# A planner in place of a hand-written schedule for the long convolutions and matrix-memory heads of an encoder layer

## The chip, the cores and the metric

The kernel runs on one core of a Trainium2 chip, in one launch. The metric is the device time of an execution in microseconds; lower is better.

## The reference

The layer normalises its input, projects it, and splits the result in a bidirectional gated long convolution of order 2 (512 channels) and a bidirectional mLSTM with four heads of 128; both go through one output projection, and a gated MLP follows. It is applied to a prompt of 1024 tokens and a sample of 512. The stage that the change touches computes `hyena_mix` and `mlstm_bidir`:

```
def hyena_mix(x1, x2, v, kspec, bias):
    def long_conv(z, ks, d):
        zf = jnp.fft.rfft(z, n=2 * L, axis=1)
        return jnp.fft.irfft(zf * ks[None], n=2 * L, axis=1)[:, :L] + d * z
    z = x1.astype(F32) * long_conv(v.astype(F32), kspec[:, 0], bias[0])
    return x2.astype(F32) * long_conv(z, kspec[:, 1], bias[1])

def mlstm_chunkwise(q, k, v, ig, fg):          # forwards, and once more on the flipped sequence
    a = b_last[..., None] - b + ig
    w_loc = jnp.exp(a - m_loc[..., None])
    kw = k * w_loc[..., None]
    C_loc = jnp.einsum('bhcsk,bhcsv->bhckv', kw, v)
    ...                                        # states C, n are carried from chunk to chunk
    Sm = jnp.einsum('bhctd,bhcsd->bhcts', q, k) * jnp.exp(D - m_t[..., None])
    num = inter[..., None] * jnp.einsum('bhctk,cbhkv->bhctv', q, C_prev) + jnp.einsum('bhcts,bhcsv->bhctv', Sm, v)
    h = num / jnp.maximum(jnp.abs(den), jnp.exp(-m_t))[..., None]
```

The heads are then normalised, multiplied by the gate `o`, and joined with the convolution's output.

## The kernel before, in words

Three stages follow one another. `projections_filters_and_gates` (L434) makes the input projection, the filters' spectra and the gates. `long_convolutions_and_heads` (L1397) is the middle stage. `output_and_mlp` (L2130) does the rest. The first and last order their work with `plan()` (L365), a list scheduler: of several streams of steps it takes at each point the step that can start first by stated costs.

**The convolutions.** A stream `st` is a sequence and half of its 512 channels: 0 and 1 are the prompt's halves (8 blocks of 128 tokens), 2 and 3 the sample's (4 blocks). Each stream goes twice, as round `o` 0 and 1, through one transform; (o, st) is a turn. In a turn:
- `split` (TensorE, L1823, one per block) makes the first part of the transform from `mix_z`, ScalarE copies it to `mix_split` (L1925), and SyncE issues a DMA that shuffles it into `mix_classes` (L1680).
- A `pair` (8 of them for a prompt half, 4 for a sample half) is `forward` (TensorE, L1835), the product with a filter block `mix_kf` (VectorE, three operations, L2009 to L2011; the blocks are loaded by SyncE, L1657, in a ring of three), `inverse` (TensorE, L1846) and a copy to `mix_classes` (ScalarE, L1930). The inverse runs two pairs behind the forward (`lag`).
- After a turn's last copy SyncE shuffles back to `mix_split`, one DMA per block (L1686).
- `join` (TensorE, L1856) and the product with the gate (VectorE, L2019, into `mix_z`; `finish`) end each block. Round 0 goes on with the splits of round 1; round 1 with `turn`, a transposition on TensorE (L1864), a copy on ScalarE (L1942) and a store to `y_scratch` on ScalarE's queue (L1950).

Buffers `z`, `split` and `classes` exist in two slots; the prompt's halves use slot 0 one after the other, the sample's halves share slot 1. The first stage loads z of stream 0, 2 and 3 ahead. z of stream 1 is loaded (`load_z`) when stream 0 is transposed.

**The heads.** There are eight jobs, each of the four heads for the sample (short) and the prompt (long). `load_head` is five loads (SyncE, L1710 to L1714); GpSimd adds the mask (L1799); ScalarE takes exponentials (`weigh_tile`, L1962); `keys` on TensorE transposes k and multiplies q by k (L1876, L1881), four tiles at a time; ScalarE scales the keys (L1973), VectorE weighs the scores (L2032); `link` (TensorE, L1892) and `add_state` (VectorE, L2047 and L2049) carry the states from chunk to chunk; `attend` (TensorE, L1905 and L1906), `age` (ScalarE, L1983) and `combine` (VectorE, L2062 and L2064) make the output; a chain on VectorE normalises it, `turn_head` (L1914) transposes, `scale` (L2111) multiplies and `store_head` (L1728) stores.

**What sets the order.** The eight PSUM banks `vyacc` are taken in turn, in the order of the schedule. A hand-written list, `schedule`, gives one joint order, which every engine follows for its own part: ScalarE's copy of a split, SyncE's shuffle of it and VectorE's product of a forward stand where the `split` or `forward` stands. The turns run (0,0), (0,2), (0,3), (1,0), (1,2), (1,3), (0,1), (1,1); `turn_at` says after which pair a turn is joined; joins and the splits or turns after them alternate at a distance of two blocks. The heads' steps are spread among these by a share of cost, with `gap` credits where the convolutions would stand:

```
        else:
            schedule.append((x[0],) + x[2:])
            credit += share * x[1] if n >= leading else 0
        while at < len(heads) and spent < credit:
            schedule.append((heads[at][0],) + heads[at][2:])
            spent += heads[at][1]
            at += 1
```

Loads hang on steps: a filter block on a `forward`, a gate on a turn's last `join`, the eight output weight blocks (`load_out_weights`, L1734, for the next stage) on the forwards of the last turn, the first outputs for the next stage on the last but one `store_head`.

## Time and profile before

| | us |
|---|---|
| median of 3 runs | 2239.07 (2234.37 to 2241.76) |
| the profiled execution | 2236.85 |
| its span | 2235.0 |
| middle stage on TensorE, first split to last transposition | 726.37 to 1085.05 |

The span lies within the execution's own time; the rest lies around it. TensorE was granted 0.985 of its full clock in the mean over the span. In the rows below TensorE has two parts, PE for matmuls and PEld for the load of weights, which overlaps them; DVE is VectorE, ACT ScalarE, POOL GpSimd, SP SyncE, and a q behind an engine's name is its sequencer or DMA queue. L and a number is a line of the kernel.

### The profile page before, as it was taken

What the parts mean: (1) busy time and instruction counts of PE and PEld (TensorE: products, weight loads), DVE (VectorE), ACT (ScalarE), POOL (GpSimd) and SP (SyncE); (2) the same over time, 40 slices, a digit from 0 to 9 for tenths busy, and PEclk for the clock granted to TensorE, in tenths of its full rate; (3) what the DMA queues carried; (4) which work ended last, traced back from release to release, by engine and by line L of the source; (5) the groups of instructions that cost most, each with busy time, mean ns of one, the idle gap of its engine ahead of it and who ended that gap; (6) DMA issues with size and microseconds to landing.
All of it is one profiled execution on the core that took longest, in us unless ns stands there. A gap on an engine that the chain in (4) does not pass through costs nothing. (4 is left out here: it accounts for less than half of the span.)

```text
span 2235.0 us, 26984 instructions
## 1 busy us (share of the span) xinstructions
PE 2139.8 (96%) x9878; PEld 1775.1 (79%) x9878; DVE 1517.8 (68%) x2078; ACT 934.1 (42%) x1482; POOL 379.4 (17%) x350
## 2 busy tenths in 40 slices
PE   6999999999999899898799999999999999999998
PEld 5788878887877788787688878888888888888886
DVE  6577677555754378577546876569999999655554
ACT  5432233325543445455325543344444444442342
POOL 0221122100110101000000056312353433100000
PEclk9999999999999899899999999999999999999999
DMA  4344444553663866758735278633334443866553
GB/s 152 109 141 139 130 130 131 160 155 133 207 195 118 256 182 208 217 166 236 254 111 191 99 257 302 220 116 107 132 137 141 141 137 104 270 232 195 172 161 118
DMA packets 239164, 377.93 MB, mean 169 GB/s; under 512 B 17816, under 2 KB 143384, under 8 KB 239034
## 3 DMA queue, kind: packets, MB, share of 16 engines
q1 hardware_dynamic: 217802, 300.70, 43.6%
q0 software_dynamic: 19936, 72.10, 8.7%
q10 hardware_dynamic: 1296, 3.41, 0.4%
q8 instruction: 80, 1.31, 0.2%
q14 instruction: 50, 0.41, 0.1%
HBM read 252.08 MB, written 98.11 MB: 157 GB/s over the span
## 5 line engine op out<-in xcount | busy, mean ns | idle before, releaser
L128 PE MATMUL in_acc<-in_h_hi,in_w_hi 128*128 128x512 f32 x464 | 191.0, 412 | 2.6 <-DVE in_h_lo L1175 2.6
L130 PE MATMUL in_acc<-in_h_hi,in_w_lo 128*128 128x512 f32 x464 | 182.0, 392 | 0.0
L129 PE MATMUL in_acc<-in_h_lo,in_w_hi 128*128 128x512 f32 x464 | 181.5, 391 | 0.0
L128 PE MATMUL mlp_bank<-down_d_hi,down_s_hi 128*128 128x512 f32 x462 | 179.7, 389 | 0.0
L129 PE MATMUL mlp_bank<-down_d_lo,down_s_hi 128*128 128x512 f32 x462 | 179.7, 389 | 0.0
L130 PE MATMUL mlp_bank<-down_d_hi,down_s_lo 128*128 128x512 f32 x462 | 179.7, 389 | 0.0
L1057 ACT ACTIVATE in_w_hi<-in_w_raw 128x1024 fp32r<-128x1024 f32 x58 | 61.5, 1060 | 214.5 <-PE in_acc L130 214.3
L128 PE MATMUL mlp_bank<-mlp_s_hi,up_w_hi 128*128 128x512 f32 x352 | 138.8, 394 | 3.1 <-DVE up_w_lo L2956 3.1
L129 PE MATMUL mlp_bank<-mlp_s_lo,up_w_hi 128*128 128x512 f32 x352 | 138.2, 393 | 0.0
L130 PE MATMUL mlp_bank<-mlp_s_hi,up_w_lo 128*128 128x512 f32 x352 | 138.0, 392 | 0.0
L2882 ACT ACTIVATE down_s_hi<-down_s_raw 128x1408 fp32r<-128x1408 f32 x42 | 58.0, 1382 | 167.2 <-PE mlp_bank L130 167.2
L1181 DVE TENSOR_TENSOR in_w_lo<-in_w_raw,in_w_hi 128x1024 fp32r<-128x1024 f32 x58 | 71.1, 1226 | 70.3 <-ACT in_w_hi L1057 70.1
L128 PEld LDWEIGHTS in_acc<-in_h_hi,in_w_hi 128*128 128x128 f32 x464 | 87.8, 189 | 20.8 <-DVE in_h_lo L1175 2.8
L128 PE MATMUL mlp_bank<-mlp_h_hi_t,wide_hi_s 128*128 128x512 f32 x264 | 102.7, 389 | 0.0
L129 PE MATMUL mlp_bank<-mlp_h_lo_t,wide_hi_s 128*128 128x512 f32 x264 | 102.7, 389 | 0.0
L130 PE MATMUL mlp_bank<-mlp_h_hi_t,wide_lo_s 128*128 128x512 f32 x264 | 102.7, 389 | 0.0
L130 PEld LDWEIGHTS in_acc<-in_h_hi,in_w_lo 128*128 128x128 f32 x464 | 87.4, 188 | 19.2
L129 PEld LDWEIGHTS in_acc<-in_h_lo,in_w_hi 128*128 128x128 f32 x464 | 87.8, 189 | 17.4
L130 PEld LDWEIGHTS mlp_bank<-down_d_hi,down_s_lo 128*128 128x128 f32 x462 | 86.7, 188 | 18.2
L128 PEld LDWEIGHTS mlp_bank<-down_d_hi,down_s_hi 128*128 128x128 f32 x462 | 86.7, 188 | 18.0
L1846 PE MATMUL mix_vyacc<-mix_prod,mix_tab 128*128 128x256 f32 x384 | 95.3, 393 | 5.8 <-DVE mix_prod L2011 5.8
L129 PEld LDWEIGHTS mlp_bank<-down_d_lo,down_s_hi 128*128 128x128 f32 x462 | 86.7, 188 | 17.8
(298 smaller groups left out, 5522.4 us busy)
## 6 DMA issues: line engine op xcount, KB each, us to landing
in_w_raw<-arg_w_in_t SPq DMA_DIRECT2D x58, 512.0 KB, 3.6
down_s_raw<-s_scratch SPq DMA_DIRECT2D x42, 704.0 KB, 4.5
up_w_raw<-arg_w_up_t SPq DMA_DIRECT2D x44, 512.0 KB, 3.6
wide_raw<-arg_w_up_t SPq DMA_DIRECT2D x44, 512.0 KB, 3.7
filt_tab<-arg_fwd SPq DMA_DIRECT2D x32, 512.0 KB, 3.8
mix_classes<-mix_split SPq DMA_DIRECT2D x48, 256.0 KB, 8.9
mix_kf<-k_scratch SPq DMA_DIRECT2D x48, 256.0 KB, 4.4
mix_split<-mix_classes SPq DMA_DIRECT2D x48, 256.0 KB, 5.2
```

Source lines behind the costliest of these rows:

```text
L128: pe.matmul(out, w_hi, x_hi, start=first, stop=False, skip_group_check=joins)
L129: pe.matmul(out, w_hi, x_lo, start=False, stop=False, skip_group_check=joins)
L130: return pe.matmul(out, w_lo, x_hi, start=False, stop=last, skip_group_check=joins)
L1057: act.activation(w_hi[b][:, :, :], raw[b][:, :, :], ACT.Copy).then_inc(sem["w_high"], 1)
L1181: dve.tensor_tensor(w_lo[b][:, :, :], raw[b][:, :, :], w_hi[b][:, :, :].bitcast(F32), ALU.subtract).then_inc(sem["w_low"], 1)
L1846: last = pe.matmul(out[:, u, :], tab[s][:, t, u, 1 + i, :], prod[g % 2][:, u, i, :], start=i == 0, stop=i == 1)
L2882: act.activation(s_hi[i % n_own][:, :, :], s_raw[i % 2][:, :, :], ACT.Copy).then_inc(sem["s_high"], 1)
```

## The change

`plan()` gets two more arguments: `takes`, which names for a step the steps that free the PSUM banks it takes, so that a step waits for the bank that was taken eight before, and `rank_of`, which decides between steps that can start at the same time. The middle stage then has no hand-written schedule. Each engine's part is a step of its own with an engine, a time, a delay and the steps that it needs (`work`), in 33 streams; `order`, what `plan()` makes of them, takes the place of `schedule`, and each engine follows its own steps in it. A step of the heads goes before one of the convolutions unless their share is ahead by more than 0.1; on SyncE the convolutions go first.

The turns run in another order (`runs`): the sample halves, the first prompt half, both sample halves' second round, then four pairs of the first prompt half's second round, the eight pairs of the second prompt half's first round, the other four pairs, and the second half's second round. Stream 0 moves to slot 1, stream 1 to slot 0, which the sample halves have first; so `load_z` waits for the transpositions of streams 2 and 3, and the first shuffle of stream 1 for their stores. The first stage's loads ahead follow that. The output weights are loaded when stream 0 is stored and four pairs are left. What each step computes is not changed, nor the number of matmuls of the stage. The ring of filter blocks, the lag and the banks stay. The diff, cut:

```diff
-def plan(streams, work, even=False):
-    clock, done, order, at = {}, {}, [], [0] * len(streams)
+def plan(streams, work, even=False, rank_of=None, takes=None, banks=8):
...
+            if takes:
+                needs = needs + [held[i - banks] for i in range(len(held), len(held) + len(takes(step))) if i >= banks]
             if all(x in done for x in needs):
                 start = max([clock.get(engine, 0.0)] + [done[x] for x in needs])
-                rank = at[n] / len(stream) if even else 0
+                rank = rank_of(n, at, step) if rank_of else at[n] / len(stream) if even else 0
...
+        held += takes(step) if takes else []
...
-                        st, s, half, z = ((0, 0, 0, ahead.z[0]), (2, 1, 0, ahead.z[1][:, 0:nts[1], :]), (3, 1, 1, ahead.z[1][:, nts[1]:, :]))[n - z_from]
+                        st, s, half, z = ((0, 0, 0, ahead.z[1]), (2, 1, 0, ahead.z[0][:, 0:nts[1], :]), (3, 1, 1, ahead.z[0][:, nts[1]:, :]))[n - z_from]
...
-    turns = [(0, 0), (0, 2), (0, 3), (1, 0), (1, 2), (1, 3), (0, 1), (1, 1)]
+    early = n_pairs[0] // 2
+    runs = [(0, 2, 0, n_pairs[2]), (0, 3, 0, n_pairs[3]), (0, 0, 0, n_pairs[0]), (1, 2, 0, n_pairs[2]), (1, 3, 0, n_pairs[3]),
+            (1, 0, 0, early), (0, 1, 0, n_pairs[1]), (1, 0, early, n_pairs[0]), (1, 1, 0, n_pairs[1])]
+    turns = [(0, 2), (0, 3), (0, 0), (1, 2), (1, 3), (0, 1), (1, 0), (1, 1)]
+    pairs = [(o, st, t) for o, st, first, end in runs for t in range(first, end)]
...
-    turn_at = {(0, 0): 12, (0, 2): 16, (0, 3): 20, (1, 0): 28, (1, 2): 32, (1, 3): 36}
+    sharers = {0: [x for x in turns if x[1] < 2], 1: [x for x in turns if x[1] >= 2]}
...
-    def join_all(o, st):
-        nb = len(blocks(st))
-        for b in range(nb + 2):
-            if b < nb:
-                conv.append(("join", 0.9, o, st, b))
-            if b >= 2:
-                conv.append(("split", 0.9, 1, st, b - 2) if o == 0 else ("turn", 0.3, st, b - 2))
-        if o == 1:
-            conv.append(("store", 0, st))
...
-    conv.append(("gap", 3.2))
-    alone = first_pair[0, 1]
-    for g in range(alone):
-        pair_step(g, alone)
-        for turn in turns:
-            if turn_at.get(turn) == g:
-                join_all(*turn)
-                if turn == (1, 0):
...
+        if kind == "load_z":
+            return "SP", 2.8, 4.0, [last_block("turn", 2), last_block("turn", 3)]
+        if kind == "split":
+            o, st, b = a
+            return "PE", 0.87, 0.1, [("finish", 0, st, b)] if o else [("load_z", 1)] if st == 1 else []
+        if kind == "shuffle":
+            o, st, b = a
+            return "SP", 0.72, 3.5, [("copy_split",) + a] + ([last_block("back", 0, st)] if o else [("store", 2), ("store", 3)] if st == 1 else [])
+        if kind == "load_k":
+            return "SP", 0.72, 3.5, [("multiply", a[0] - ring)] if a[0] >= ring else []
+        if kind == "forward":
+            o, st, t = pairs[a[0]]
+            return "PE", 0.87, 0.1, [last_block("shuffle", o, st), ("load_k", a[0])] + ([("inverse", a[0] - lag)] if a[0] >= lag else [])
+        if kind == "multiply":
+            return "DVE", 2.1, 0.1, [("forward", a[0]), ("load_k", a[0])] + ([("inverse", a[0] - 2)] if a[0] >= 2 else [])
...
+        if kind == "join":
+            return "PE", 0.87, 0.1, [("back",) + a, ("load_gate",) + a[:2]]
+        if kind == "load_gate":
+            same = sharers[0 if a[1] < 2 else 1]
+            n = same.index(a)
+            return "SP", 2.8 * nts[streams[a[1]][0]] / 8, 4.0, [last_block("finish", *same[n - 1])] if n else []
...
+        if kind == "load_head":
+            j = a[0]
+            return "SP", 6.8 * size, 4.0, [last_tile("attend", j - 2)] if j >= 2 else []
+        if kind == "add_mask":
+            return "POOL", 5.0 * size, 0.1, [("load_head", a[0])]
+        if kind == "weigh_tile":
+            return "ACT", 0.78 if a[1] else 2.1, 0.1, [("add_mask", a[0])]
+        if kind == "keys":
+            j, i = a
+            return "PE", 1.31, 0.1, [("weigh_tile", j, quad * i + quad - 1)] + ([("link", j - 1, len(tiles_of(j - 1)) - 2)] if j else [])
...
+        if kind == "attend":
+            return "PE", 0.9, 0.1, [last_quad("weigh", a[0]), last_link(a[0])]
...
+        if kind == "load_wo":
+            return "SP", 1.4, 4.0, [("store", 0), ("forward", len(pairs) - 4)]
+        return "SP", 1.4, 4.0, [("store_head", len(jobs) - 2), ("store", 2), ("store", 3), ("store", 0)]
+    def takes(step):
+        kind, a = step[0], step[1:]
+        release = {"split": ["copy_split"], "forward": ["multiply"], "inverse": ["copy_classes"], "join": ["finish"], "turn": ["copy_turned"],
+                   "keys": ["scale_keys", "weigh"], "link": ["add_state"], "attend": ["combine", "combine"], "turn_head": ["scale"]}
+        return [(x,) + a for x in release.get(kind, [])]
...
+    conv_streams = [by_turn("join", turns), [("turn", st, b) for st in outer_turns for b in blocks(st)], by_turn("split", split_turns),
+                    [("inverse", g) for g in all_pairs], [("forward", g) for g in all_pairs]]
+    head_streams = [by_quad("keys"), [x for j in all_jobs for x in [("link", j, i) for i in tiles_of(j)[1:]] + [("attend", j, i) for i in tiles_of(j)]
+                                      + [("turn_head", j, i) for i in quads_of(j)]]]
+    head_streams[1] = [(x[0], x[1], x[2] - 1) if x[0] == "link" else x for x in head_streams[1]]
...
+    def rank_of(n, at, step):
+        conv = step[0] in conv_kinds
+        if work(step)[0] == "SP":
+            return 0.0 if conv else 1.0
+        some = range(len(conv_streams)) if conv else range(len(conv_streams), len(costs))
+        share = sum(costs[i][at[i]] for i in some) / sum(costs[i][-1] for i in some)
+        return share + 0.1 if conv else share
...
-    for step in schedule:
+    for step in order:
...
-            return (0, 0) if st < 2 else (1, (st - 2) * big // 2)
+            return (1, 0) if st == 0 else (0, 0 if st == 1 else (st - 2) * big // 2)
...
+                    if g >= ring:
+                        sp.wait_ge(sem["multiplied"], g - ring + 1)
...
-                    if st == 1:
-                        sp.wait_ge(sem["transposed"], t_at[0, len(blocks(0)) - 1] + 1)
+                    for old in (2, 3):
+                        sp.wait_ge(sem["transposed"], t_at[old, len(blocks(old)) - 1] + 1)
...
-                        sp.wait_ge(y_stored[0], 16 * (HC // P))
+                        for old in (2, 3):
+                            sp.wait_ge(y_stored[old], 16 * (HC // P))
...
-                load_head(0)
-                for step in schedule:
-                    kind, args = step[0], step[1:]
-                    if kind == "split":
-                        shuffle_classes(*args)
-                        if args == (0, 0, nts[0] - 1):
-                            for g in range(ring):
-                                load_k(g)
-                        if args == (0, 3, nts[1] - 1):
-                            load_head(1)
-                            load_gate(0, 0)
-                            load_o(0)
-                            load_gate(0, 2)
-                            load_o(1)
...
-                    elif kind == "forward":
-                        load_after(*args)
-                        if pairs[args[0]][:2] == (1, 1):
-                            load_out_weights(pairs[args[0]][2])
...
+                run({"shuffle": shuffle_classes, "load_k": load_k, "back": shuffle_split, "load_gate": load_gate, "load_z": load_z,
+                     "load_head": load_head, "load_o": load_o, "store_head": store_head, "load_wo": load_out_weights, "load_so": load_first_outputs})
...
+                run({"copy_split": copy_split, "copy_classes": copy_classes, "copy_turned": copy_turned, "store": store_turned,
+                     "weigh_tile": weigh_tile, "scale_keys": scale_keys, "age": age, "magnitude": magnitude, "root": root})
```

The lines of the changed kernel for the same operations are: split L1845, forward L1857, inverse L1868, join L1878, turn L1886, keys L1898 and L1903, link L1914, attend L1927 and L1928, turn_head L1936.

What moved is seen at three places on TensorE; a count at a row's end is of instructions, of which the trace's rows have two records each (so a forward, a join or a split is four records and an inverse eight). The first is the third long head, from its last links (L1892, now L1914) to its first attend (L1905, now L1927). Before:

```order
L1892 MATMUL mix_vyacc<-mix_v,mix_keys 128x129 x2
L1846 MATMUL mix_vyacc<-mix_prod,mix_tab 128x256 x4
L1892 MATMUL mix_vyacc<-mix_v,mix_keys 128x129 x4
L1835 MATMUL mix_vyacc<-mix_classes,mix_tab 128x256 x2
L1892 MATMUL mix_vyacc<-mix_v,mix_keys 128x129 x2
L1856 MATMUL mix_vyacc<-mix_split,mix_otab 128x256 x2
L1905 MATMUL mix_vyacc<-mix_state,mix_q 128x129
L1906 MATMUL mix_vyacc<-mix_v,mix_e 128x129
```

Now:

```order
L1914 MATMUL mix_vyacc<-mix_v,mix_keys 128x129 x14
L1857 MATMUL mix_vyacc<-mix_classes,mix_tab 128x256 x2
L1898 MATMUL mix_vyacc<-all_ident,mix_k 128x128 x4
L1903 MATMUL mix_vyacc<-mix_q,mix_k 128x128 x4
L1857 MATMUL mix_vyacc<-mix_classes,mix_tab 128x256 x2
L1868 MATMUL mix_vyacc<-mix_prod,mix_tab 128x256 x4
L1878 MATMUL mix_vyacc<-mix_split,mix_otab 128x256 x4
L1927 MATMUL mix_vyacc<-mix_state,mix_q 128x129
L1928 MATMUL mix_vyacc<-mix_v,mix_e 128x129
```

The links stand together, and a forward, the next head's first keys, a forward, an inverse and two joins stand between the last of them and the first attend, where there was one join.

The second place is where z of the second prompt half is first used, by the splits (L1823, now L1845). Before, they follow on pairs of the samples' second round, with head work ahead:

```order
L1846 MATMUL mix_vyacc<-mix_prod,mix_tab 128x256 x4
L1835 MATMUL mix_vyacc<-mix_classes,mix_tab 128x256 x2
L1823 MATMUL mix_vyacc<-mix_z,mix_otab 128x256 x16
L1876 MATMUL mix_vyacc<-all_ident,mix_k 128x128 x4
L1881 MATMUL mix_vyacc<-mix_q,mix_k 128x128 x4
```

Now:

```order
L1878 MATMUL mix_vyacc<-mix_split,mix_otab 128x256 x4
L1886 MATMUL mix_vyacc<-all_ident,mix_z 128x128 x6
L1868 MATMUL mix_vyacc<-mix_prod,mix_tab 128x256 x4
L1886 MATMUL mix_vyacc<-all_ident,mix_z 128x128 x2
L1857 MATMUL mix_vyacc<-mix_classes,mix_tab 128x256 x2
L1868 MATMUL mix_vyacc<-mix_prod,mix_tab 128x256 x4
L1845 MATMUL mix_vyacc<-mix_z,mix_otab 128x256 x14
```

The transpositions of a sample half (L1886), whose end now allows the load of that z, stand one forward and one inverse ahead of the splits.

The third place is TensorE's end of the stage in the changed kernel:

```order
L1857 MATMUL mix_vyacc<-mix_classes,mix_tab 128x256 x2
L1868 MATMUL mix_vyacc<-mix_prod,mix_tab 128x256 x8
L1936 MATMUL mix_vyacc<-all_ident,mix_state 128x128 x8
L1878 MATMUL mix_vyacc<-mix_split,mix_otab 128x256 x16
L1886 MATMUL mix_vyacc<-all_ident,mix_z 128x128 x16
```

Behind the last two inverses stand the last head's two `turn_head` (L1936), then all eight joins, then all eight turns. Before, the last head's attends stood between the last inverse and the first join, and joins and turns alternated.

## Rows read from the trace of the kernel before

**Rows 1.** The page, busy time, share of the span and instructions of each engine:

```profile
PE 2139.8 (96%) x9878; PEld 1775.1 (79%) x9878; DVE 1517.8 (68%) x2078; ACT 934.1 (42%) x1482; POOL 379.4 (17%) x350
```

**Rows 2.** The middle stage's window: length, busy (count) of five engines, PEclk, DMA, GB/s:

```profile
726.00:1086.00 360.00, 314.35 (x1712) 275.06 (x1712) 238.53 (x476) 174.31 (x448) 29.79 (x18) 0.94 0.71 207
```

**Rows 3.** TensorE's waits, 726 to 1086: us in all, times, longest:

```profile
PE mix_vyacc L1905 <- issue: 11.0, 8, 3.9
PE mix_vyacc L1835 <- issue: 10.6, 2, 7.6
PE mix_vyacc L1823 <- DVE mix_z L2019: 5.9, 3, 2.9
PE mix_vyacc L1846 <- DVE mix_prod L2011: 5.8, 2, 5.1
...
PE mix_vyacc L1892 <- ACT mix_keys L1973: 3.7, 2, 2.7
PE mix_vyacc L1864 <- DVE mix_z L2019: 3.1, 3, 1.8
PE mix_vyacc L1823 <- DMA mix_z<-tok_scratch: 2.9, 1, 2.9
PE mix_vyacc L1914 <- DVE mix_state L2101: 1.3, 1, 1.3
```

**Rows 4.** Windows at half clock, TensorE alone; the last one, and all eight's sum:

```profile
1088.60:1095.40 6.80, 3.19 (x8) 0.50 1.03 301
sum 47.60, PE 34.21; mean PE 4.28
```

**Rows 5.** Timeline, 893 to 905: start, length, instruction [idle before, its releaser]:

```profile
899.74 0.69 DVE L2009 TENSOR_TENSOR mix_prod<-mix_vyacc,mix_kf 128x512 f32<-128x512 f32 x1 [1.81 <-DMA mix_kf<-k_scratch]
...
902.58 0.77 PE L1905 MATMUL mix_vyacc<-mix_state,mix_q 128*128 128x129 f32 x2 [3.91 <-issue]
```

**Rows 6.** DMA issues, 726 to 1090: count, KB each, median us to landing:

```profile
mix_classes<-mix_split SPq DMA_DIRECT2D x48, 256.0 KB, 8.9
mix_kf<-k_scratch SPq DMA_DIRECT2D x48, 256.0 KB, 4.4
mix_split<-mix_classes SPq DMA_DIRECT2D x48, 256.0 KB, 5.2
...
mix_z<-tok_scratch SPq DMA_DIRECT2D x1, 1024.0 KB, 11.9
```

**Rows 7.** DMA issues of stretches: 804 to 826, 726 to 760, 1050 to 1080:

```profile
mix_classes<-mix_split SPq DMA_DIRECT2D x8, 256.0 KB, 3.2
mix_gate<-tok_scratch SPq DMA_DIRECT2D x1, 1024.0 KB, 8.5
...
mix_classes<-mix_split SPq DMA_DIRECT2D x16, 256.0 KB, 10.3
...
mix_split<-mix_classes SPq DMA_DIRECT2D x8, 256.0 KB, 4.9
```

**Rows 8.** Groups by line and form, ScalarE: its table loads at the exponentials:

```profile
L1962 ACT ACT_TABLE_LOAD x8 | 10.3, 1283 | 0.1
```

**Rows 9.** Timeline at the stage's start and end; last a window, columns as in 2:

```profile
726.37 15.74 PE L1823 MATMUL mix_vyacc<-mix_z,mix_otab 128*128 128x256 f32 x64 [4.51 <-PEq L119]
...
1059.30 1.79 SPq L1734 DMA_DIRECT2D out_raw_w<-arg_w_out_t  x2
...
1063.87 1.89 PE L1846 MATMUL mix_vyacc<-mix_prod,mix_tab 128*128 128x256 f32 x8
...
1066.43 8.47 SPq L1686 DMA_DIRECT2D mix_split<-mix_classes  x8
...
1071.41 2.75 PE L1856 MATMUL mix_vyacc<-mix_split,mix_otab 128*128 128x256 f32 x12
...
1092.21 0.77 PE L128 MATMUL mlp_bank<-out_w_hi,out_s_hi 128*128 128x512 f32 x1 [7.16 <-DVE out_w_lo L2924]
...
1062.00:1066.00 4.00, 3.09 (x20) 2.92 (x21) 1.29 (x5) 1.13 (x4) 0.00 (x0) 1.00 1.01 340
```

More of the change, by code:

```diff
@@ L1428, in outwards @@
         return [x for i in range(nt // 2) for x in (nt // 2 - 1 - i, nt // 2 + i)]
-    conv = []
-    def split_all(o, st):
-        conv.extend([("split", 0.9, o, st, b) for b in blocks(st)])
-    def pair_step(g, count):
-        if g - lag >= 0 and (g - lag) < len(pairs):
-            conv.append(("inverse", 1.8, g - lag))
-            for o, st in turns:
-                if last_pair[o, st] == g - lag:
-                    conv.append(("back", 0, o, st))
-        if g < count:
-            conv.append(("forward", 0.9, g))
@@ new lines, in long_convolutions_and_heads @@
+    conv_kinds = ("join", "turn", "split", "inverse", "forward", "multiply", "finish", "copy_split", "copy_classes", "copy_turned", "store",
+                  "shuffle", "load_k", "back", "load_gate", "load_z", "load_wo", "load_so")
+    def rank_of(n, at, step):
[5 more added lines that the diff above has]
+        return share + 0.1 if conv else share
@@ L1640, in gate_of @@
         def gate_of(o, st):
-            i = slot(st)[0]
-            same = [x for x in turns if slot(x[1])[0] == i]
-            return i, same.index((o, st))
+            i = 0 if st < 2 else 1
+            return i, sharers[i].index((o, st))
         def run(handlers):
-            for step in schedule:
+            for step in order:
                 if step[0] in handlers:
@@ L2112, in scale @@
                                              ALU.mult, ALU.mult).then_inc(sem["scaled"], 1)
[L2114 to L2115 removed]
+                run({"multiply": multiply, "finish": finish, "weigh": weigh, "add_state": add_state, "combine": combine, "shares": shares,
+                     "weight": weight, "add": add, "square": square, "reduce": reduce, "unit": unit, "scale": scale})
 PRODUCTS = ("p1", "p6", "p2", "p7", "p5", "p4", "p3")
```

235 lines of the change are left out of this document (114 added, 121 removed).

## The prediction

> **What bounds the kernel now.** I read the busy shares first: TensorE is busy 96% of the span and everything else far less [rows 1], so only TensorE's time counts, and of that only what it spends waiting or at the lower clock. Then the windows by stage: in the middle stage, which alone the change touches, TensorE is busy 314.35 of 360 us at a mean granted clock of 0.94 [rows 2]. On TensorE the stage goes from 726.37 us to the end of the last transpositions at 1085.05 (the next matmul starts at 1092.21 after 7.16 us idle), 358.7 us [rows 9]. Its waits there, one row per kind [rows 3], sum to 11.0 + 10.6 + 5.9 + 5.8 + 3.7 + 3.1 + 2.9 + 1.3 = 44.3 us (the 4.51 us ahead of the first matmul is the change of stage and stays [rows 9]). Three of these kinds end with a DMA: 10.6 ("issue" before L1835, where the operand `mix_classes` is written by a DMA) and 2.9 for `mix_z`, 13.5 us together. The other 30.8 us are waits for VectorE and ScalarE. At half clock (0.50, the 1.2 GHz level) TensorE was busy 34.21 - 3.19 = 31.0 us in this stage, in seven windows, each beside one of the waits (the last row lies beyond the stage) [rows 4]. Work takes twice as long there, so this cost 15.5 us. The floor that waits and clock leave is 358.7 - 44.3 - 15.5 = 299 us.
>
> How a wait arises is seen at 902.58 [rows 5]: the first matmul of a head's `attend` needs every state of that head; VectorE, which adds the states, was at 899.74 held 1.81 us by a filter block (`mix_kf`) that SyncE had issued late, and then multiplied a pair before the last states. TensorE stood 3.91 us and then ran at half clock.
>
> **The change, part by part.** The matmuls are the same in number and form. What moves is the order on every engine, each now from its own step's planned time. I price each kind of wait by how much TensorE work the new order puts between a release and its user. Durations: 12 records of 128x256 take 2.75 us and 8 take 1.89, so four more cost 0.86 [rows 9]; I use 0.87 for a forward, join or split (four records) and 1.73 for an inverse (eight).
>
> - Attend after link. Before, the eight heads have 0 to 1.7 us of TensorE work between last `link` and first `attend`. Now they have 2.2 to 6.5 us: at the third long head it was one join (0.87) and is now forward 0.87, keys 1.33, forward 0.87, inverse 1.73, two joins 1.73. The 11.0 us fall to 1: saves 10.
> - Joins first, splits after them, instead of alternating at a lag of two, and turns after joins: 5.9 + 3.1 + 1.3 fall to 1: saves 9.3.
> - Keys before link: 3.7 falls to 1.5, by the same reading: saves 2.2.
> - The start. The sample goes first, so the 2.9 us part of L1835 goes: 12 splits (10.4 us) now lie between the first sample half's last split and its first forward. Pairs then run with no head work until head 0 is loaded, and each product (three VectorE operations like that of 0.69 us [rows 5], 2.07 us) lies open in part: 1.7 + 0.7 + 1.5 + 0.6 = 4.5, in place of 5.8. Head 0's five loads are issued after all 16 shuffles instead of ahead of them; the cover is six pairs, 15.6 us, and I charge 2. Saves 1.3 - 2 = -0.7, with the 2.9 counted next.
> - Forward after split, for the two turns of the second prompt half. A shuffle needs the copy (0.7) and issue (0.7), and lands after 8.9 us in the median [rows 6], after 3.2 in a quiet stretch and 10.3 in a crowded one [rows 7]. The new order has 4.4 us and 5.3 us of cover there, so the wait is between 0.2 and 7.3 at one and 0 and 6.4 at the other. I take a landing of 6, since a 1 MB gate or z load and little else is ahead: 3 each. 10.6 falls to 6: saves 4.6. (The planner counts 3.5 us for this landing.)
> - z of the second half. It may be loaded once the sample halves are transposed. Ahead of the load stand five loads of the next head, and between the last turn and the first split TensorE has a forward and an inverse, 2.6 us. A 1 MB load lands after 8.5 us [rows 7] or, this very one, 11.9 us [rows 6]: the wait is 6.2 to 9.6. I take 8, where it was 2.9: costs 5.1.
> - Join after inverse. Cover is 3.5 us at the second sample half and 4.4 at the first prompt half; needed are 0.7 + 5.2 [rows 6]: costs 2.4 + 1.5 = 3.9. Bounds 0 and 7.
> - The tail. Before, the last head's attends filled the 5.6 us between the last inverse (1065.8) and the first join (1071.41) [rows 9]. Now only two `turn_head` (0.9 us) do. Copy 0.7, landing 4.9, the eight shuffles at 1.06 us each (8.47 us for 8 [rows 9]), the last join 0.9, its product 0.6 and eight turns, now all behind the joins, 1.8: 16.3 us with 9.6 of work in it: costs 6.7. Bounds 4 and 10.
> - ScalarE loads its table six times less often (16 loads before, eight of them with the exponentials of L1962, 1283 ns each [rows 8]). ScalarE is busy 174 of 360 us [rows 2], so I price this at nothing; were ScalarE the releaser, it would be worth up to 8.
> - Filter blocks: same 48 loads in the same ring of three. Planned on their own they no longer queue behind `gate` and `head` loads by hand rule, but may behind waits planned too early. Bounds -2 and +4; I take 0, as their landing, 4.4 us [rows 6], fits in two pairs (5.2 us).
>
> Sum of idle: -10 - 9.3 - 2.2 + 0.7 - 4.6 + 5.1 + 3.9 + 6.7 = -9.7. The half-clock windows follow the longer waits: seven before, 2.2 us each on average; I see six after (stage entry, start, z, two forwards, tail), -2. Together -11.7 on the profiled execution's 2236.85 us (span 2235.0): 2225.2. The median of the runs shown lies 2.2 us higher, 2239.07, so I forecast **2227.5 us**. The measurement tells about 0.3%, 6.7 us, from no change.
>
> What could speak against it in the tail: SyncE now issues seven of the eight output weight blocks and the outputs of a tile (512 KB each, 4.2 MB) in one go, 8.7 us (four inverses, two forwards) ahead of the last eight shuffles. If what was issued first is moved first, then at the 340 GB/s of a saturated stretch [rows 9] this takes 12.3 us, and the first join comes 3.6 us later: 2231.1 us. In the trace of before 1 MB of weights was issued 7.1 us ahead of those shuffles (1059.30 and 1066.43), and the first join still ran within 5.0 us of the first shuffle's issue [rows 9], so I charge nothing. The Trainium skill (DMA: Bandwidth & Descriptors, Queues, rings and completion order) has the rule: on each DMA engine the descriptors of a queue are consumed in ring order. By it the time would be the 2231.1 us, by the row 2227.5; the trace doesn't contradict it, since 1 MB had passed by then.
>
> **The rivals.**
> 1. Slower: the transfers land as in the crowded rows, and the planner, which counts 3.5 to 4 us, has left no cover. Forwards 13.7 instead of 6 (+7.7), z +1.6, tail +3.6 (the weights ahead), joins +2.4 (shuffles back queue behind shuffles out), first heads +4, two more half-clock windows +5: +24.3, **2252 us**. Each microsecond of landing counts about five times (two forwards, z, two joins), so it decides from landings 2.3 us later than I took them, 8.3 us for a shuffle. For it: the median of 8.9. Against: the crowd of the start, where the median is 10.3 [rows 7], is thinner now with the head loads issued after the shuffles, and the gate load no longer sits among them.
> 2. No difference: the engine waits move rather than go. ScalarE now does 16 exponentials of a long head in one piece (6.2 us and a table load) and VectorE's product of keys waits for them, with pair products queued behind it on VectorE; then TensorE stands at the inverse. If half of the 21.5 us saved on engine waits comes back so, the time is **2238 us**. For it: both orders are in sequence on each engine, and nothing steps past a late one. Against: the plan gives this chain 20 us or more after each head's loads, except one.
> 3. Better: landings are quick (3.2 us) because the crowd at the start is gone. Forwards 0.5, z 6.2, joins 1, first heads 0 saves another 12.2, and three fewer half-clock windows 6.6: **2208.7 us**.
> 4. The weights first in the tail, as worked out above, all else as forecast: **2231.1 us**.
>
> The change does what it says: the new order does show the sample first and the second half's pairs between two groups of four pairs of the first half's second round.
>
> **How the numbers follow.** My forecast has 0.38, quick landings 0.14, the weights alone 0.10, moved waits 0.20, late landings 0.18. The forecast's own range is 2219 to 2236, and part of it (above 2232.4) counts as no change. Faster by over 0.3%: 0.38 and 0.14 and half of the 0.10, less the tenth of my forecast's part, 0.04, that lies above that line, some 0.54; within: 0.27; slower: 0.19. The range goes from quick landings to most of late ones, 2207 to 2248.
>
> **What would show it.** Stage length on TensorE (first split to last turn) near 347 us; waits at the first matmul of attend near 1 us; one wait of 6 to 10 us for `mix_z`; a wait of 4 to 8 us at the last round's first join, with a half-clock window; forwards of stream 1 waiting 2 to 4 us twice. I am wrong if VectorE or ScalarE still make TensorE wait 15 us or more, if shuffles land after more than 8 us in the second half of the stage, or if the next stage's first matmul comes more than 8 us after the last turn (now 7.16 [rows 9]), the weights being late.

## The result: slower by half a per cent, and the profile after

The changed kernel takes 2251.09 us (median of 11 runs, 2246.37 to 2256.49) against 2240.74 us for the kernel before in the same comparison (11 runs, 2234.37 to 2246.52): ratio 1.0054, 95% interval 1.0043 to 1.0066. The forecast was 2227.5 us, and its range ended at 2248. The medians differ by 10.4 us; the two profiled executions (2236.85 and 2250.08 us, spans 2235.0 and 2248.2) by 13.2.

First the busy time of the engines over the span, and the windows of the middle stage (columns as in [rows 2]; the second window ends with the stage now):

```profile
PE 2140.6 (95%) x9878; PEld 1772.4 (79%) x9878; DVE 1521.2 (68%) x2078; ACT 924.8 (41%) x1476; POOL 383.0 (17%) x350
```

```profile
726.00:1086.00 360.00, 304.76 (x1662) 264.31 (x1663) 237.77 (x466) 161.84 (x426) 32.79 (x18) 0.95 0.70 202
726.00:1100.00 374.00, 315.85 (x1712) 273.30 (x1712) 242.57 (x476) 163.93 (x436) 32.79 (x18) 0.95 0.70 201
```

TensorE does the same 1712 matmul records in 315.85 us that took 314.35 [rows 2]; nearly all that it loses, it loses by standing. Now its waits, from 720 to 1120 us (us in all, times, longest), which answer to [rows 3]:

```profile
PE mix_vyacc L1868 <- DVE mix_prod L2033: 31.8, 20, 4.9
PE mix_vyacc L1878 <- DMA mix_split<-mix_classes: 8.8, 5, 2.8
PE mix_vyacc L1857 <- issue: 8.2, 2, 6.6
PE mlp_bank L128 <- DVE out_w_lo L2946: 7.9, 1, 7.9
PE mix_vyacc L1845 <- PEq L119: 4.5, 1, 4.5
PE mix_vyacc L1936 <- DVE mix_state L2123: 2.4, 1, 2.4
PE mix_vyacc L1845 <- DMA mix_z<-tok_scratch: 2.1, 1, 2.1
PE mix_vyacc L1936 <- ACT mix_classes L1952: 1.3, 1, 1.3
PE mix_vyacc L1878 <- DVE mix_state L2071: 1.0, 1, 1.0
...
PE mix_vyacc L1927 <- DVE mix_state L2071: 0.3, 1, 0.3
```

The last matmuls of the stage on TensorE's timeline, and the first of the next:

```profile
726.75 15.47 PE L1845 MATMUL mix_vyacc<-mix_z,mix_otab 128*128 128x256 f32 x64 [4.52 <-PEq L119]
...
1081.02 1.99 PE L1868 MATMUL mix_vyacc<-mix_prod,mix_tab 128*128 128x256 f32 x8 [1.39 <-DVE mix_prod L2033]
1085.39 1.09 PE L1936 MATMUL mix_vyacc<-all_ident,mix_state 128*128 128x128 f32 x8 [2.38 <-DVE mix_state L2123]
1088.55 7.72 PE L1878 MATMUL mix_vyacc<-mix_split,mix_otab 128*128 128x256 f32 x28 [2.06 <-DMA mix_split<-mix_classes]
1096.52 1.13 PE L1878 MATMUL mix_vyacc<-mix_split,mix_otab 128*128 128x256 f32 x4 [0.25 <-DMA mix_split<-mix_classes]
1097.49 1.91 PE L1886 MATMUL mix_vyacc<-all_ident,mix_z 128*128 128x128 f32 x16
1107.33 0.77 PE L128 MATMUL mlp_bank<-out_w_hi,out_s_hi 128*128 128x512 f32 x1 [7.94 <-DVE out_w_lo L2946]
```

The stage runs from 726.75 to 1099.40, 372.65 us; it was 358.7. Its waits sum to 56.7 us (the two of the table at the stage's borders left out, four small ones of 0.2 to 0.3 left in), and were 44.3: 12.4 more. What is left over the floor of 299 us is 17 us for the half clock, and was 15.5. So 12.4 + 1.5 makes the stage's 14 us, 13.2 of which reach the span.

The wait for attend is gone (11.0 to 0.3), as are those for keys and for joins and splits in large part. But one row has grown from 5.8 to 31.8 us: TensorE at an inverse (L1868) waits for the product of its pair on VectorE (L2033). In both kernels the longest of these waits is for a filter block, 5.08 us before and 4.94 now, so the open products themselves went from 0.8 to 26.9 us. The timeline of VectorE, GpSimd and TensorE shows how:

```profile
820.35 1.89 PE L1857 MATMUL mix_vyacc<-mix_classes,mix_tab 128*128 128x256 f32 x8
...
823.62 1.99 PE L1868 MATMUL mix_vyacc<-mix_prod,mix_tab 128*128 128x256 f32 x8 [1.38 <-DVE mix_prod L2033]
...
826.23 1.23 DVE L2104 TENSOR_TENSOR mix_state<-mix_state,mix_rden 128x1024 f32<-128x1024 f32 x1
826.32 1.93 PE L1868 MATMUL mix_vyacc<-mix_prod,mix_tab 128*128 128x256 f32 x8
827.49 0.69 DVE L2031 TENSOR_TENSOR mix_prod<-mix_vyacc,mix_kf 128x512 f32<-128x512 f32 x1
828.19 0.68 DVE L2032 TENSOR_TENSOR mix_prod<-mix_vyacc,mix_kf 64x512 f32<-64x512 f32 x1
828.89 0.69 DVE L2033 TENSOR_TENSOR mix_prod<-mix_vyacc,mix_kf 64x512 f32<-64x512 f32 x1
829.62 1.23 DVE L2104 TENSOR_TENSOR mix_state<-mix_state,mix_rden 128x1024 f32<-128x1024 f32 x1
829.64 1.99 PE L1868 MATMUL mix_vyacc<-mix_prod,mix_tab 128*128 128x256 f32 x8 [1.39 <-DVE mix_prod L2033]
830.88 1.23 DVE L2108 TENSOR_TENSOR mix_state<-mix_state 128x1024 f32<-128x1024 f32 x1
830.99 6.61 POOL L1825 TENSOR_TENSOR mix_e<-mix_e,mix_mask 128x1024 f32<-128x1024 f32 x2 [33.24 <-DMA mix_v<-tok_scratch]
831.47 1.89 PE L1857 MATMUL mix_vyacc<-mix_classes,mix_tab 128*128 128x256 f32 x8
832.14 3.25 DVE L2112 TENSOR_TENSOR mix_state<-mix_state 128x1024 f32<-128x1024 f32 x1
835.42 0.69 DVE L2031 TENSOR_TENSOR mix_prod<-mix_vyacc,mix_kf 128x512 f32<-128x512 f32 x1
...
837.57 3.78 PE L1868 MATMUL mix_vyacc<-mix_prod,mix_tab 128*128 128x256 f32 x8 [4.21 <-DVE mix_prod L2033]
```

Pairs stand alone on TensorE here: a forward and an inverse, 2.6 us, then the next. There are two losses. The first is cover: at the first pair of such a group only one forward, 0.87 us, lies between the pair's own forward and its inverse, against a product of 2.07 us, and TensorE waits 1.38 us (at 823.62). The second is VectorE's queue: between two products it puts one operation of the last head's normalisation (L2104, L2108, L2112), 1.23 us, so that it needs 3.3 us a pair and sets the pace. The square (L2112) took 3.25 us beside GpSimd's mask and made one wait of 4.21. In a later group of eight the pace is seen by itself, 3.38 us from one inverse to the next:

```profile
911.40 1.99 PE L1868 MATMUL mix_vyacc<-mix_prod,mix_tab 128*128 128x256 f32 x8 [0.53 <-DVE mix_prod L2033]
...
914.78 1.99 PE L1868 MATMUL mix_vyacc<-mix_prod,mix_tab 128*128 128x256 f32 x8 [0.53 <-DVE mix_prod L2033]
...
918.16 1.99 PE L1868 MATMUL mix_vyacc<-mix_prod,mix_tab 128*128 128x256 f32 x8 [0.52 <-DVE mix_prod L2033]
```

A count says how often the order leaves a product uncovered: the TensorE work between a pair's forward and its inverse, worked out from each kernel's order with the durations of [rows 9]. Before, 1 of 48 pairs has less than the product's 2.1 us there; now 15 have, ten of them 0.9 or less. Before, head work and pairs were mixed by hand, and the longest group of inverses with only forwards between was four; now there are two of eight and two of six.

### The profile page after: what moved, and what is told of

Its sections match the earlier page's. It is cut to its first block and busy times, and to the rows that moved or that the text cites. A ratio compares the mean times of both kernels' runs of the same rounds, so it can differ in the third digit from the quotient of the medians.

```text
span 2248.2 us, 26979 instructions
## 1 busy us (share of the span) xinstructions
PE 2140.6 (95%) x9878; PEld 1772.4 (79%) x9878; DVE 1521.2 (68%) x2078; ACT 924.8 (41%) x1476; POOL 383.0 (17%) x350
## 5 line engine op out<-in xcount | busy, mean ns | idle before, releaser
L1868 PE MATMUL mix_vyacc<-mix_prod,mix_tab 128*128 128x256 f32 x384 | 100.0, 407 | 32.0 <-DVE mix_prod L2033 31.8
L1868 PEld LDWEIGHTS mix_vyacc<-mix_prod,mix_tab 128*128 128x128 f32 x384 | 74.7, 201 | 51.0 <-DVE mix_prod L2033 41.0
```

The source lines that it names most:

```text
L1868: last = pe.matmul(out[:, u, :], tab[s][:, t, u, 1 + i, :], prod[g % 2][:, u, i, :], start=i == 0, stop=i == 1)
```

## Experiments

Theory A: the planner is greedy. It takes at each moment a step that can start, heads first up to a lead of 0.1 of the work, so head work bunches, and the pairs that are left stand alone with their products and VectorE's normalisation open. Theory B: the dealt pairs and swapped slots cost the time. Theory C: the transfers land later than the planner says. Ratios are to the kernel before, in the same comparison, with their 95% intervals.

**1. The planner with the old turns.**

```diff
-    runs = [(0, 2, 0, n_pairs[2]), (0, 3, 0, n_pairs[3]), (0, 0, 0, n_pairs[0]), ...
+    runs = [(o, st, 0, n_pairs[st]) for o, st in ((0, 0), (0, 2), (0, 3), (1, 0), (1, 2), (1, 3), (0, 1), (1, 1))]
-            return (1, 0) if st == 0 else (0, 0 if st == 1 else (st - 2) * big // 2)
+            return (0, 0) if st < 2 else (1, (st - 2) * big // 2)
```

> Edit: the changed kernel's planner with the turns, buffer slots and waits of the kernel before, so without the dealt pairs. Theory A (the planner bunches a head's TensorE work, so that pairs stand alone with VectorE's normalisation between their products; products hold TensorE 31.8 us against 5.8): stays slow, product waits 20 us or more, time 2245 to 2256 us. Theory B (the dealing and the swapped slots cost the time): product waits near 6 us and a time at or under the kernel before, 2225 to 2241 us.

2259.91 us, ratio 1.0086 (1.0066 to 1.0107), 4 us over theory A's range. Products wait 21.2 us, none of it for a filter block, with 14 pairs under 2.1. The largest waits, and TensorE alone in the window of the stage (length, busy, PEclk, DMA, GB/s):

```profile
PE mix_vyacc L1865 <- DVE mix_prod L2030: 21.2, 22, 2.3
PE mix_vyacc L1854 <- issue: 13.4, 2, 7.5
...
PE mix_vyacc L1842 <- DMA mix_z<-tok_scratch: 6.4, 1, 6.4
```

```profile
726.00:1110.00 384.00, 324.19 (x1712) 0.93 0.67 195
```

Theory B falls: planning alone, with the turns of before, makes the kernel some 19 us slower than the hand-written order, and the new turns and slots win 7 (by the ratios) to 9 (by the medians) of these back. They do so by the clock: the waits of this run's stage sum to 58.5 us, near the 56.7 of the changed kernel, but the two of the forwards (7.5 and 5.9) and that of z (6.4) are long, and TensorE is busy 324.19 us for the records that it did in 315.85, 8.3 us more at the lower level.

**2. The normalisation on an eighth of its columns.**

```diff
-                    return state[:, 0:nts[jobs[j][1]], d, 0:HD]
+                    return state[:, 0:nts[jobs[j][1]], d, 0:HD // 8]
```

> Edit: in the changed kernel the six normalisation operations of each head on VectorE work on 16 of the 128 columns (this leaves out seven eighths of the head normalisation); every order stays. Long heads then put about 0.2 us between two products, not 1.23. Theory A: the waits of 0.53 us in a row and half of the 4.21 us ones go, product waits fall from 31.8 to 12 to 18 us (the 1.38 us at each group's first pair and the 4.94 us for a filter block stay), time 2232 to 2239 us. Theory C (late transfers are what costs): no more than 5 us less, 2246 us or above.

2239.04 us, ratio 0.9997 (0.9984 to 1.0009), 12 us under the changed kernel. Products 21.8 us, 10 less; the two waits of 4.21 us fell to 1.4 each, and in place of the three of 0.53 in the group of eight there is one of 1.23, at a product that stands for a filter block. The time is at the upper end of what was expected and the products' row above it: the uncovered products, which the edit leaves as they are, make most of the 16.9 us that are left beside the first filter block's 4.9, more than the expectation had counted. The joins' waits rose from 8.8 to 12.9. So VectorE's normalisation is some 10 of the 26 us that the row grew by, and the order's missing cover most of the rest. Against theory C's 5 us at most, 12.

**3. The mask on one tile.**

```diff
-                        part = e[d][:, first:first + nts[s], :]
+                        part = e[d][:, first:first + 1, :]
```

> Edit: in the changed kernel GpSimd adds the mask to one tile of a head, not to all (this leaves the mask out of the other tiles); every order stays. The square of a long head on VectorE took 3.25 us beside a mask addition and 1.22 us elsewhere. Theory of contention between the two engines: the square falls to 1.22 us at both places, the two waits of 4.21 us fall to about 2.2, time 4 us less, 2247 us. Rival: the long square has another cause (a hidden wait in its chain) and stays at 3.25 us, time the same within 1.5 us. By theory A alone contention is a small part of the 26 us.

2242.46 us, ratio 1.0017 (1.0001 to 1.0033), 8.6 under the changed kernel, twice what was expected. The square is back near its own time:

```profile
829.61 2.79 POOL L1825 TENSOR_TENSOR mix_e<-mix_e,mix_mask 128x128 f32<-128x128 f32 x2 [33.21 <-DMA mix_v<-tok_scratch]
830.73 1.36 DVE L2112 TENSOR_TENSOR mix_state<-mix_state 128x1024 f32<-128x1024 f32 x1
```

Both waits of 4.21 us fell to 2.32, and products to 28.9 in all (-2.9); joins wait 5.5 (-3.3), and TensorE is busy 313.54 us instead of 315.85, less of it at half clock (-2.3). That makes the 8.55 us by which the next stage begins earlier in the profile. The ten times lie between 2239.10 and 2252.01 us and the profiled one is the shortest of them, so how far the 8.6 us exceed the expected 4 is loose. The first part is the contention itself: 3.8 us at the two places. Whether the joins are its follower or come from the exponentials, which start at 832.43 and not at 837.63, this run doesn't tell. Contention is real, and small beside 26 us.

**4. No lead for the heads.** The rule that breaks ties returns `share` for both kinds.

> Edit: in the changed kernel's planner the heads lose their lead of 0.1 of the work over the convolutions when both can start at once. Theory A: head and pair work alternate more finely, product waits fall to 15 to 22 us; what they give may be lost again at the end, where less head work is done early (turn_head waits for the last normalisation), so 2235 to 2250 us. Rival (the lead is what feeds the long chain of a head, and without it heads come late): product waits the same, time above 2255 us.

2258.13 us, ratio 1.0079 (1.0057 to 1.0101). Products fell to 20.0 us (11 pairs under 2.1), as theory A has it, though the time didn't fall: `turn_head` now waits 10.5 us and the joins 13.7: the long chain of each head comes late. The expected 2235 to 2250 was missed; the time is the one that the rival gave (above 2255), with theory A's product waits. Product waits can be traded for others with nothing won.

**5. Offsets to the planner's choice.** From here on orders were searched: a replay of an order with durations measured in the traces scored the orders of some thousands of offsets.

```diff
+                key = start + lead.get(step[0], 0)
-                if best is None or (start, rank) < best[:2] or ...
+                if best is None or (key, rank) < best[:2] or ...
+        share += wave.get(step[0], 0)
```

> Edit: the changed kernel with its turns, buffers, streams, costs and delays, but the planner's choice between ready steps has offsets by kind of step (a lead in us before starts are compared, and an addition to the rank), found by replaying many orders with durations measured in the traces; that replay gives 341 us for the stage where it gives 372 for the changed kernel (372.7 measured). Theory A (only the choice between ready steps, which lets pairs stand alone, costs the time): product waits fall from 31.8 to 12 to 18 us, and the time to 2225 to 2238 us. Theory C (transfers): the same waits for DMA, 19 us, remain and the time stays above 2245 us. If the replay is wrong about what matters, no gain.

2250.43 us, ratio 1.0051 (1.0036 to 1.0066): no gain, though products fell to 15.2 us. The chain of the stage's end says why:

```profile
1084.31 0.33 SPq L1791 DMA_DIRECT2D y_scratch<-mix_og  x1
...
1084.68 4.24 SPq L1796 DMA_DIRECT2D out_raw_w<-arg_w_out_t  x8
...
1107.30 0.77 PE L128 MATMUL mlp_bank<-out_w_hi,out_s_hi 128*128 128x512 f32 x1 [21.30 <-DVE out_w_lo L2952]
```

The stage ended at 1086.0, 13.4 us earlier than in the changed kernel, but SyncE had the last `store_head` ahead of the weights, and that waited for the last head. The next stage began at the same time as before the edit (1107.33). The replay had scored the end of TensorE's stage alone, and that too well: it gave 341 us where the stage took 360, so of 31 us promised there 13 came.

**6 and 7. A third product buffer, forwards three pairs ahead of inverses**; in 6 with searched offsets (six early pairs; shuffles, filter blocks and shuffles back planned to land after 5 us), in 7 alone:

```diff
-    lag, ring = 2, 3
+    lag, ring = 3, 3
-        prod = [p.sb(f"prod{b}", [P, 2, 2, HC]) for b in range(2)]
+        prod = [p.sb(f"prod{b}", [P, 2, 2, HC]) for b in range(3)]
```

> Edit: as the tuned order, with a third product buffer and forwards three pairs ahead of inverses, six early pairs and the shuffles planned to land after 5 us; the replay gives 336 us for the stage. Theory A: product waits 4 to 10 us, since a late product can be made up for over one pair more; time 2218 to 2235 us. If the buffer adds nothing beyond the order, equal to the tuned order within 3 us.

> Edit: the changed kernel with a third product buffer and forwards three pairs ahead of inverses (the planner told so), nothing else. Theory A in its strict form (VectorE's rate: 2.07 us of product and 1.23 us of normalisation a pair against 2.6 us on TensorE): more distance does not help where the rate is the limit, product waits stay 22 us or more, time within 5 us of 2251. Rival (the distance is too short: each group's first product lies open for 1.38 us, seven times): product waits fall to under 20 us and the time to 2240 us or less.

6: 2227.18 us, ratio 0.9943 (0.9925 to 0.996), products 6.1 us, 5.5 of it for a filter block, 3 pairs under 2.1: as expected. 7: 2244.83 us, ratio 1.002 (1.0009 to 1.0032), products 26.5 us, 12 pairs under 2.1: theory A's waits, with the time 1 us outside its 5, and far from the rival's 2240 and less. More distance alone is worth 6 us: the greedy order still spends it, and where VectorE needs 3.3 us a pair it must.

**8. Later landings in the plan.** The shuffles of splits are planned at 8.0 us, z at 9.

> Edit: the changed kernel's planner is told that a shuffle lands after 8.0 us, not 3.5, and the load of z after 9 us, not 4. Theory C (planned landings too early are the cost): the waits for shuffles (8.2 us) and z (2.1 us) nearly go, time 2240 us or less. Theory A: these 10 us of waits fall by half at best, products stay at 25 us or more and the time moves by less than 5 us.

2244.95 us, ratio 1.0031 (1.0017 to 1.0044). Waits for shuffles 5.3 (from 8.2), z 2.2 (2.1), products 30.2. The move is 6 us (5 by the ratios), at the edge of what theory A allowed, and far from explaining the result: of theory C a small part holds.

**9. The order of 5 with the weights ahead of the last store_head**, on SyncE alone.

> Edit: the tuned order of e5, in which only SyncE's order changes: the eight output weight blocks and the next stage's first outputs are issued ahead of the last store_head, which waits for the last head, not behind it. In e5 the stage on TensorE ended at 1086.0 (1099.4 in the changed kernel), but the next stage's first matmul stood 21.3 us, to 1107.3, for weights and outputs issued at 1084.7 and after. Theory (the gain of the middle stage was real, and a load queued behind a wait on SyncE gave it back): the wait falls to 8 to 12 us and the time to 2236 to 2242 us. Rival (the loads land late whatever their place, since y_scratch must be stored first): wait above 16 us, time above 2245 us.

2244.84 us, ratio 1.0028 (1.0016 to 1.0041). The next stage's wait is 17.0, not 21.3 and not 8 to 12; the wait is as the rival has it, the time just under its 2245. The stage itself ended 5 us earlier. The weights now stand behind the eight shuffles back, which SyncE issued from 1060.14 to 1070.69, and then SyncE waits for the store of the first half's result:

```profile
SPq L1796 <- DMA y_scratch<-mix_classes: 4.6, 1, 4.6
```

They go out at 1075.35. In both runs the next stage's first matmul comes 22.6 us after the first block's issue (1084.68 and 1107.30; 1075.35 and 1097.95): its start follows the issue of these loads, and moved with it by the same 9.3 us. What is left of the delay is the 10.55 us behind the shuffles and the 4.6 for the store.

**10 and 11. Searched again**, with a replay that also counts the next stage's loads, the contention of GpSimd and VectorE and the half clock, over four sets of durations.

> Edit: as e6 (third product buffer, forwards three pairs ahead, offsets to the planner's choice), the offsets searched again with a replay that also counts the next stage's loads, the GpSimd contention and the half clock, over four sets of durations; mean 349 us where e6 has 357 and the changed kernel 389. Theory A with the replay right: 4 to 8 us under e6, 2219 to 2224 us. If the replay's rest is noise: equal to e6, 2223 to 2231 us.

> Edit: as e10, another searched set of offsets (five early pairs, shuffles planned to land after 4 us), mean 351 us in the replay. Expected like e10, 2219 to 2228 us; product waits under 12 us. If it is over 2235 us, the replay doesn't carry over from one order to another and the gain of e6 was a lucky order.

10: 2222.56 us, ratio 0.9926 (0.9908 to 0.9944), products 12.2 us, 6.0 of it for a filter block. 11: 2220.09 us, ratio 0.9917 (0.9899 to 0.9935), products 9.9 us, 5.9 of it for one filter block; this beats both kernels, by 18 and 31 us. Both times lie where they were expected. The largest waits of 11 inside the stage:

```profile
PE mix_vyacc L1863 <- issue: 11.6, 2, 8.4
PE mix_vyacc L1874 <- DVE mix_prod L2039: 9.9, 6, 5.9
PE mix_vyacc L1884 <- DMA mix_split<-mix_classes: 4.8, 3, 3.4
```

And the same normalisation of a long head as above, on VectorE and TensorE:

```profile
910.88 7.17 PE L1851 MATMUL mix_vyacc<-mix_z,mix_otab 128*128 128x256 f32 x32 [0.41 <-DMA mix_z<-tok_scratch]
...
913.27 2.36 DVE L2110 TENSOR_TENSOR mix_state<-mix_state,mix_rden 128x1024 f32<-128x1024 f32 x2
915.66 1.23 DVE L2114 TENSOR_TENSOR mix_state<-mix_state 128x1024 f32<-128x1024 f32 x1
916.92 1.23 DVE L2118 TENSOR_TENSOR mix_state<-mix_state 128x1024 f32<-128x1024 f32 x1
917.89 5.34 PE L1874 MATMUL mix_vyacc<-mix_prod,mix_tab 128*128 128x256 f32 x24
```

VectorE runs the chain beside splits, which need nothing of it, and three products were ready before, so that three inverses (24 records) follow one another without a wait.

**12. 10 with two product buffers.**

> Edit: e10 with its searched offsets, but two product buffers and forwards two pairs ahead as in the changed kernel, and the planner told so. If the offsets carry the gain over the changed kernel (2251 to 2222.6 us), it stays under 2232 us with product waits under 18 us. If it is the third buffer and the greater distance, product waits rise to 25 us or more and the time to 2240 us or above; the replay gives 361 us for the stage where it gives 337 to 340 for e10. If offsets and distance only work together (the choice of every later step shifts when one condition changes), likewise 2240 us or above, although the third buffer alone was worth 6 us (e7).

2259.45 us, ratio 1.0083 (1.0065 to 1.01), products 26.4 us, 13 pairs under 2.1. This is the third expectation: neither the offsets nor the distance carries the gain alone; offsets belong to the one plan for which they were searched. The replay gave 361 us for this stage, below the 372 of the changed kernel; it took 384, so the replay misled here too.

## Why the prediction was wrong, step by step

**The step that failed** is in the part on the start: "Pairs then run with no head work until head 0 is loaded, and each product ... lies open in part: ... 4.5, in place of 5.8". The row measured 31.8 us, 26 more than before where I had 1.3 less. The step failed in three ways.

First, the 5.8 us were misread. 5.08 of them end with a DMA, since VectorE itself stood for a filter block:

```profile
768.57 0.69 DVE L2009 TENSOR_TENSOR mix_prod<-mix_vyacc,mix_kf 128x512 f32<-128x512 f32 x1 [6.25 <-DMA mix_kf<-k_scratch]
...
770.72 3.78 PE L1846 MATMUL mix_vyacc<-mix_prod,mix_tab 128*128 128x256 f32 x8 [5.08 <-DVE mix_prod L2011]
```

Open products cost 0.8 us before, and the filter block's wait stayed, 4.94; I let 4.5 us of open products take the place of both. (By the same reading, 5.08 of the 30.8 us that the prediction gives to VectorE and ScalarE are a DMA's.)

Second, the mechanism was there, but priced for one stretch only. The same rule, TensorE work between a pair's forward and its inverse against the product's 2.07 us, applied to all 48 pairs of the new order gives 15 open ones, 14.6 us in sum (an estimate from the durations of [rows 9]); experiment 2, which takes the normalisation nearly away, leaves 16.9 (1.2 of it for another filter block). The order was at hand.

Third, the rule takes VectorE to be free for a product when its forward ends. It had the last head's normalisation in its queue, 10 us by experiment 2, 3.8 of them from the contention with GpSimd. No term of the sum had this. Without that term the forecast had -8.4 us of waits (-9.7 + 1.3), and the trace has -13.6 (12.4 - 26): the rest of the sum was right in sign and too small, with misses on both sides that cancel in part:

- Attend after link, 11.0 to 1: 0.3. Right. Keys, 3.7 to 1.5: under 0.9 (the small rows left out above). Right.
- Joins, splits and turns, 10.3 to 1: 4.7 (1.0, 1.3, 2.4 in the rows above). The last is the final `turn_head`, which now waits for the end of the last head's chain.
- Forward after split, 10.6 to 6: 8.2, but 1.6 and 6.6, not 3 and 3. A landing of 6 us fits neither turn: in the first the eight shuffles landed after 4.3 us in the median, in the second, issued right behind a gate load of 1 MB, after 9.4 (window 1022 to 1031):

```profile
mix_classes<-mix_split SPq DMA_DIRECT2D x8, 256.0 KB, 9.4
```

- z of the second half, 2.9 to 8: 2.1. The load landed after 8.8 us, near the lower of the two landings taken (8.5 and 11.9); the cover, 2.6 us in the count, was 6.7 in time, since the inverse in it waited 2.24 us for its product and ran at half clock. A cover that is counted at full speed is too short where its own work waits.
- Joins after inverses and the tail, +3.9 and +6.7: joins waited 6.5 us for three earlier turns and 2.3 in the tail, with `turn_head`'s 2.4 beside it. In the tail 16.3 us with 6.7 of waits were forecast; from the end of the last inverse (1083.01) to the stage's end it was 16.4 us with 4.7.
- The weights ahead of the last shuffles: the eight blocks were issued by 1075.7, the first shuffle back at 1083.68, and the first join ran 4.9 us later, as before [rows 9]. The rival of the ring order wasn't put to the test: the shuffles came 12.5 us after the first of the seven blocks (1071.20), and it gives these transfers 12.3.
- Half clock, -2: +1.5.
- ScalarE's tables and the filter blocks, both priced at nothing: no change seen; the first block that is loaded into a used place of the ring is waited for 4.94 us (5.08 before).

Of the signs of being wrong, the first came true (VectorE makes TensorE wait 15 us or more), the second for one turn of two (9.4 us), the third not (7.94 us, and 8 were allowed).

Of the rivals, the second had the place, "TensorE stands at the inverse", and named VectorE's queue, but tied it to late exponentials and gave it 10.75 us at most, no more than had been won elsewhere. Nothing in it reads the size off the order. The first, late landings, gave 2252 us, within 1 us of the measured time, by luck: the waits that it adds up didn't come, save for one turn's forward (forwards 8.2 us where it has 13.7, z 2.1 where it has 9.6), and planning for late landings (experiment 8) wins 6 us.

One more reading would have warned beforehand: the planner's own clock. Run over its own order with its own costs, it shows 27.9 us of idle TensorE before inverses, where 26.9 were measured without the filter block. That it is so near is luck in part: for the order of run 1 the plan has 34.8 and the trace 21.2. But it tells good orders from bad: 3.0, 8.5 and 6.0 us in the plans of runs 6, 10 and 11, and 22.7 or more for the changed kernel and runs 1, 7, 8 and 12. So the loss lay in the order as planned, not in costs that were far off; a greedy choice doesn't look at what it leaves for later.

## What to carry to other kernels

When an order is planned anew, count the cover of every release and user pair over the whole stage, before and after, on the engine that bounds it, and not only at the waits that the old profile shows: a wait that is small there may be small because the old order hid it. A greedy list scheduler fills the bounding engine now and leaves the pairs that need another engine to stand alone; read its own idle time before trusting it. Beside the cover, ask what else the engine that makes the product has in its queue at that point. And judge an order by the start of the next stage, not by the end of its own.

## What the runs showed of the hardware

A two-operand operation on VectorE with both operands in SBUF took 3.25 us beside GpSimd's addition of the mask, and 1.23 us elsewhere; GpSimd's two additions then took 6.61 us, and 4.66 alone (912.69). With the mask on one tile the same operation took 1.36 us. The products, whose one operand is in PSUM, kept 0.69 us throughout. The Trainium skill (SBUF — State Buffer, SBUF: two separate sides) says that the two engines share a port pair as an exclusive lock for such operations, and the one that comes second waits for the whole instruction. The rows agree, and the two engines take turns: the first addition (830.99 to 834.31) began within L2108 and took 3.32 us, not 2.35; the square began at 832.14, within that addition, and ended 1.08 us after it; the second addition (834.27 to 837.60) began within the square and again took 3.33. I hadn't priced it, although the kernel before has an addition of 5.67 us in place of 4.66.
